# A wider pitch and another start for the input tiles of a TensorE-bound layer, with half the reserve in front

## The reference

```
h = h + 0.5 * swiglu(rms_norm(h, norm_ffn1), gate1, up1, down1)      # 2048 -> 5632 -> 2048
h = h + mixer(rms_norm(h, norm_mix))                                 # HGRN2 and S5 branches
h = h + 0.5 * swiglu(rms_norm(h, norm_ffn2), gate2, up2, down2)
return rms_norm(h, norm_final)[:, 16:]

swiglu(x, g, u, d) = (silu(x @ g) * (x @ u)) @ d
mixer: proj = u @ w_in (9216 + 1536 columns); a gated linear recurrence of 12 heads,
       a diagonal state-space layer; two projections to 2048, gated and merged, @ w_out
```

## Time and profile before

| what | value |
|---|---|
| median of 3 runs | 2297.54 us (2297.49 to 2297.95) |
| span of the profiled execution | 2296.0 us, 1.5 us less than the median |
| TensorE matmuls | 2288.4 us busy, 17,054 of them |
| VectorE, ScalarE, GpSimd busy | 67%, 46%, 9% of the span |
| TensorE clock granted | 1.000 (mean over the core's span) |
| read from memory | 405.48 MB, 178 GB/s over the span |

### The profile page before, as it was taken

The page is one execution under the profiler, slowest core; times in us unless marked ns, Lnnn a source line. Parts: engine busy times, 40 slices in busy tenths (PEclk is TensorE's granted clock), DMA queues, the critical chain, the costliest instruction groups (busy, mean ns, idle before and its releaser), DMA issues.

```text
span 2296.0 us, 45701 instructions
## 1 busy us (share of the span) xinstructions
PE 2288.4 (100%) x17054; PEld 2146.1 (93%) x17054; DVE 1544.2 (67%) x2143; ACT 1051.3 (46%) x1336; POOL 196.3 (9%) x267
## 2 busy tenths in 40 slices
PE   9999999999999999999999999999999999999998
PEld 9999999999999999998888899998888888888888
DVE  7555544467654589998988886567666655666654
ACT  6444333445543444445565654454444433444444
POOL 0000010289300000002000000000000000000000
PEclk9999999999999999999999999999999999999999
DMA  7555555555556555554555455656566566656564
GB/s 252 174 175 172 175 176 177 176 173 167 182 168 180 174 156 176 173 172 152 162 166 173 155 176 191 186 174 198 185 191 187 189 185 185 185 181 196 183 183 139
DMA packets 117672, 408.62 MB, mean 178 GB/s; under 512 B 17376, under 2 KB 17632, under 8 KB 117600
## 3 DMA queue, kind: packets, MB, share of 16 engines
q1 hardware_dynamic: 116880, 406.55, 57.7%
q10 hardware_dynamic: 720, 1.08, 0.1%
HBM read 405.48 MB, written 2.10 MB: 178 GB/s over the span
## 4 chain that ended last, share of the span: by engine, by line
PE 99%; ACT 0%; DVE 0%; issue 0%; POOL 0%; ACTq 0%; POOLq 0%
PE ps L423 32%; PE ps L418 31%; PE ps L422 17%; PE ps L421 16%; PE ps L644 0%; PE ps L394 0%; PE ps L651 0%; PE ps L594 0%; PE ps L583 0%; PE ps L503 0%; PE ps L637 0%; PE ps L659 0%; PE ps L661 0%; PE ps L635 0%; PE ps L663 0%; PE ps L662 0%
## 5 line engine op out<-in xcount | busy, mean ns | idle before, releaser
L1129 DVE TENSOR_TENSOR w_lo<-raw,w_hi 128x1024 fp32r<-128x1024 f32 x764 | 945.6, 1245 | 584.6 <-ACT w_hi L725 578.2
L423 PE MATMUL ps<-xs,w_lo 128*128 128x256 f32 (+2 forms) x4416 | 1256.7, 285 | 0.0
L725 ACT ACTIVATE w_hi<-raw 128x1024 fp32r<-128x1024 f32 x764 | 801.7, 1057 | 884.7 <-PE ps L423 876.9
L418 PE MATMUL ps<-xs,w_hi 128*128 128x512 f32 (+1 forms) x2432 | 857.6, 396 | 0.0
L423 PEld LDWEIGHTS ps<-xs,w_lo 128*128 128x128 f32 x4416 | 832.7, 189 | 0.0
L421 PE MATMUL ps<-xs,w_hi 128*128 128x272 f32 (+2 forms) x1984 | 572.3, 288 | 0.0
L422 PE MATMUL ps<-xs,w_hi 128*128 128x272 f32 (+2 forms) x1984 | 571.2, 288 | 0.0
L418 PEld LDWEIGHTS ps<-xs,w_hi 128*128 128x128 f32 x2432 | 457.0, 188 | 105.9 <-issue 1.6
L423 PE MATMUL ps<-hs,w_lo 128*128 (+2 forms) x1408 | 402.5, 286 | 0.0
L422 PEld LDWEIGHTS ps<-xs,w_hi 128*128 128x128 f32 x1984 | 377.1, 190 | 0.1
L421 PEld LDWEIGHTS ps<-xs,w_hi 128*128 128x128 f32 x1984 | 373.3, 188 | 0.4
(11 more groups left out here) (289 smaller groups left out, 1597.2 us busy)
## 6 DMA issues: line engine op xcount, KB each, us to landing
raw<-up SPq DMA_DIRECT2D x176, 512.0 KB, 3.7
raw<-down SPq DMA_DIRECT2D x176, 512.0 KB, 3.6
raw<-gate SPq DMA_DIRECT2D x175, 512.0 KB, 4.2
raw<-w_in SPq DMA_DIRECT2D x168, 512.0 KB, 3.6
raw<-w_out SPq DMA_DIRECT2D x32, 512.0 KB, 4.2
raw<-w_proj SPq DMA_DIRECT2D x24, 512.0 KB, 3.7
raw<-glu_a SPq DMA_DIRECT2D x8, 512.0 KB, 4.0
raw<-glu_b SPq DMA_DIRECT2D x8, 512.0 KB, 3.6
```

What stands on the lines that cost most here:

```text
L418: pe.matmul(ps[:, banks + c, 0:2 * n].rearrange("p (s t) -> p s t", s=2), hi, x, start=start and k == 0, stop=False)
L423: last = pe.matmul(out, lo, xh, start=False, stop=stop and k == KT - 1)
L725: act.activation(w_hi[:, slot, :, :], raw[:, slot, :, :], ACT.Copy).then_inc(hi_ready, 1)
L1129: tt(w_lo[:, slot, :, :], raw[:, slot, :, :], w_hi[:, slot, :, :].bitcast(f32), SUB).then_inc(lo_ready, 1)
```

## The change

Each half of an xs tile gets 288 floats (PITCH) in place of 272 (T); the 16 floats behind the values are never read or written. A new array of 32 floats stands in front of xs and another behind it. The reserve in front of all arrays is 8192 bytes in place of 16,384. `x_hi` and `x_lo` are still taken as slices of xs, and all uses of them go on reading and writing columns 0 to 271 or 16 to 271.

```diff
+PITCH = 288
+DMA_SCRATCH = 8192
...
         h = sb("h", [P, DT, T])
-        xs = sb("xs", [P, DT, 2, T], f32r)
+        sb("in_front_of_xs", [P, 32])
+        xs = sb("xs", [P, DT, 2, PITCH], f32r)
         x_hi, x_lo = xs[:, :, 0, :], xs[:, :, 1, :]
+        sb("behind_xs", [P, 32])
         gain = sb("gain", [P, 4, DT])
...
-    nc = bacc.Bacc("TRN2", target_bir_lowering=False, num_devices=1)
+    nc = bacc.Bacc("TRN2", target_bir_lowering=False, num_devices=1, dynamic_dma_scratch_size=DMA_SCRATCH)
```

## The result

The changed kernel takes **2283.36 us**, median of 5 runs (2282.81 to 2287.18), against 2297.64 us before on the same chip: a ratio of 0.9941 with a 95% interval of 0.9929 to 0.9952 (the ratios below are of the same kind, with their intervals in brackets). That is 14.3 us less. The profiled execution has a span of 2281.1 us against 2296.0, 14.9 us less.

A forecast was written before the change was run, and what follows sets the result against it. The prediction took TensorE's spacing from matmul to matmul as the bound. From a 2296.0 us span, minus 8 (narrow xs) plus 3 (wide xs) gave 2291.0, plus 1.5 outside the span 2292.5 us; range 2285 to 2305.

The forecast's parts named there:

- What bounds the kernel: Whole kernel: TensorE is busy throughout, time is the sum of steps between matmuls, and the splitting engines are early.
- Narrow steps on xs: Three-matmul steps on xs tiles: 928 of 1856 fall from 381.3 to 372.5 ns, minus 8 us; bounds 0 and plus 8.
- Wide pairs on xs: 2432 pairs of a 512- and a 256-column matmul on xs: plus 3 us; bounds minus 5 and plus 7.8.
- All other arrays: Weights, hs and all behind it move by whole steps of 256 bytes: 0, bound 2 us either way.
- The reserve: Halving the reserve in front of all arrays costs nothing, as nothing in the trace points to its use.
- The slower one: Rival, chance 0.25: wide xs pairs cost what hs pays because the second half starts further on, 7.8 us more, 2305 us.
- The no-change rival: Rival, chance 0.24: alternation comes from change-over between tiles of unlike place, even tiles' loss being odd tiles' gain; 2297.5 us.
- The much faster one: Rival, chance 0.08: most excess in the xs stages goes; a quarter of 141 us is 35 us, giving 2262 us.

The follow-up runs named there:

- a3: Kernel before with the reserve halved to 8192 and pitch 288, but no arrays around xs; 2299.10 us, ratio 1.0011.
- b1: Changed kernel with the halves of an xs tile 272 floats apart, a tile still taking 576 floats; 2289.42 us, ratio 0.9969.
- c4: Changed kernel with xs 64 bytes further on and everything else in its place; 2291.11 us, ratio 0.9971.
- a2: Kernel before with the reserve halved and both arrays of 32 floats around xs, pitch still 272; 2295.60 us, ratio 0.9991.
- a1: Kernel before with only the reserve halved, pitch 272 and no arrays around xs; 2297.65 us, ratio 0.9999.
- b2: Changed kernel with the halves still 288 floats apart but an xs tile taking 608 floats; 2282.06 us, ratio 0.9933.
- d2: Changed kernel with the halves 304 floats apart and an xs tile taking 608 floats; 2287.14 us, ratio 0.9957.
- c2: Changed kernel with gain, ones, ident, scr and the small arrays 160 bytes further on and hs 256 bytes further on; 2288.24 us, ratio 0.9959.
- a4: Changed kernel with raw, the weight tiles and h 128 bytes lower, xs and all behind it unmoved; 2298.94 us, ratio 1.0010.
- d1: Changed kernel with xs 64 bytes earlier and everything else in its place; 2293.20 us, ratio 0.9981.
- b3: Changed kernel with hs in halves of 288 floats too, and 40 more floats behind xs, moving the small arrays and hs; 2294.06 us, ratio 0.9984.
- c1: As b3, but the 40 floats directly in front of hs, so gain, ones, ident and scr lie as in the changed kernel; 2279.84 us, ratio 0.9941.

## Why the prediction was wrong

**What bounds the kernel.** Right: the step from matmul to matmul is the time, and the splitting engines are covered. ScalarE's split still waits 860.5 us for TensorE.

**Narrow steps on xs, minus 8 forecast, 6 measured.** The size was about right, the reason wrong, so the agreement is luck; and the sign of the forecast rested on this term alone. I took the alternation of 372.5 and 381 ns as the prices of the places 128 and 0. With all tiles at place 0 (a3) the narrow step is as cheap as with all at 128, and after the change the steps alternate still. What made it cheaper is padding between the halves: with a half that begins where the other ends a matmul costs 125.5 ns, at both tile pitches tried (before and b1).

**Wide pairs on xs, plus 3 forecast, minus 8.5 measured by the dense figures (7 with what the mixer keeps).** This is the step that failed. I read from two equal starts of 0.35 us that x_hi's place costs nothing, and took half of hs's disadvantage for the new gap between the halves. The gap is innocent: at the same gap the pair is at 346.6, 350.1 or 353.3 ns, by place (after, c4, a3), and at the old gap it is at 346.6 too (b1). The figure of before was not the best in the kernel to be lost, but the middle of three levels 3.3 ns apart. The bounds, -5 and +7.8, were drawn around it with too little below: 2 ns, from hs's steps, which were a rhythm and no price.

**All other arrays, 0 forecast, minus 2 measured.** Wide hs fell from 353.3 to 350.0 ns though its place modulo 256 is the same, as much as my bound. a2 has the same gain with xs at its old pitch. a2's expectation had a rival by which the distance modulo 512 decides, and before, a1, a2, a3 and after fit it. But it isn't hs's own placement alone: in c4, b2 and d2 hs lies as in the changed kernel and costs 352.9 to 353.5, and in c2 it lies modulo 512 as before and costs 350.6 (2 x 105 / 599). The bound of 2 us was worked out from some 1500 k-steps; hs, o and zs hold 1728, which leaves it at 2.

**The reserve, 0.** Right (a1).

**The rivals.** The slower one had its mechanism half right: a wide pair at 353.3 ns exists and costs the 8 us that it was priced at, but at place 0 (a3, a4), not through the gap. The no-change rival was right that only the mean of the alternation counts, but not in its cause: tiles of like place alternate as well. The much faster one was far off, but spoke rightly for more to win than the neighbouring rows show: b2's narrow steps reach 123.3 ns.

What is shown is that the distance between the input and the weights (a4, with xs fixed) and the distance of the halves (b1 against after) set the levels, and that a level also depends on what ran before (d1's and c2's two stretches, the same xs in b3, where padded narrow steps are dearer than unpadded ones). It follows that a single run at each place is no price list: b2 has both places and the best level, which the place by itself does not explain. Why a level is what it is stays open; the records show no wait between these matmuls. That the warm-up's operand chooses the rhythm was not shown either: between b3 and c1 all the small arrays moved at once, and in c2 hs too.

## What to carry to other kernels

In a stream of matmuls without waits, measure the spacing from long windows; a difference between neighbouring steps may be a rhythm and must not be priced. Padding an operand and shifting it act together: the pad alone lost 1.4 us here, the shift alone won 2 (on another array, hs), both won 14. Where TensorE is busy throughout, try some distances between moving operand and weights, look at the stages apart, and time often enough to see a second rhythm before a variant is called best.

## What the hardware showed that I had not expected

At the full granted clock the same matmul sequence holds one of a few spacings over stretches of hundreds of microseconds: a wide pair 346.6, 350.0 or 353.3 ns; 24 narrow matmuls of 272 columns some 53 ns apart (124.5 and 126.8 ns each in the first stretch of c1 and b3). Counted by the k-step the narrow levels lie as far apart as the wide ones, 3.3 ns: 3 x 210 / 1703 = 369.9 ns (b2), 373.2 (after), 376.6 (before) and 380.0 (b3). At the granted clock of 1.00 (2.4 GHz) this is eight cycles, an estimate (3.3 x 2.4). Not every stretch stands on such a level: narrow hs has 375.0, wide xs 348.0 in d2 and 352.2 in b4. Why the levels are there is open.

Two stretches of one execution with the same operands can hold different ones, and by their times so can two executions of one kernel, 2279 and 2293 us in c1. Two versions have a lower median than the changed kernel: c1, 2279.84 us but with those 2293 us in three runs of ten, and b2, 2282.06 us with all four runs within 0.3 us. b2's 1.3 us are within what the two intervals leave open.
